# The RMS factor of four dense inputs, moved from the input to the evacuation, in a decoder step on one core

## What is computed

```python
def rms_norm(x, g):
    xf = x.astype(F32)
    y = xf * lax.rsqrt(jnp.mean(xf * xf, axis=-1, keepdims=True) + EPS)
    return (y * g.astype(F32)).astype(x.dtype)

def modulate(x, g, shift, scale):
    return rms_norm(x, g) * (1.0 + scale) + shift

def swiglu_ffn(h, w13, w2):
    a, b = jnp.split(h @ w13, 2, axis=-1)
    return (jax.nn.silu(a) * b) @ w2
```

## Time and profile before

| | us |
|---|---|
| median of 3 runs | 2125.33 (2123.13 to 2126.2) |
| the profiled execution | 2127.41 |
| its span, first to last instruction | 2125.8 |
| TensorE busy | 1877.3 (88%) |
| VectorE busy | 780.2 (37%) |
| ScalarE busy | 722.0 (34%) |
| GpSimd busy | 174.3 (8%) |

### The profile page before, as it was taken

How to read it: one execution, slowest core, us unless ns; L and a number is a source line. 1 busy time by engine, 2 the same in 40 slices (tenths; PEclk the granted TensorE clock), 3 DMA queues, 4 the chain that set the end, 5 groups by cost and what they waited for, 6 DMA issues and landing times.

```text
span 2125.8 us, 43188 instructions
## 1 busy us (share of the span) xinstructions
PE 1877.3 (88%) x17058; PEld 1647.2 (77%) x17058; DVE 780.2 (37%) x1200; ACT 722.0 (34%) x1056; POOL 174.3 (8%) x321
## 2 busy tenths in 40 slices
PE   4999995999999978979878988788769599999998
PEld 1647994999999978977433767677539599999997
DVE  3993333333322333156477222222223423333222
ACT  4432333333332223244333644344111333333222
POOL 2100122000000221010010000000004200000000
PEclk9899996999999988989677999999768799999999
DMA  8775321222222221212442899899851122222222
GB/s 233 261 265 177 95 86 30 79 84 84 79 68 81 82 86 50 79 50 90 133 134 90 272 393 349 322 345 381 318 186 50 35 84 79 85 83 67 82 81 72
DMA packets 245680, 302.86 MB, mean 142 GB/s; under 512 B 10451, under 2 KB 195774, under 8 KB 245438
## 3 DMA queue, kind: packets, MB, share of 16 engines
q1 hardware_dynamic: 241504, 292.14, 41.6%
q10 hardware_dynamic: 3142, 8.11, 1.1%
q0 software_dynamic: 928, 1.06, 0.2%
HBM read 293.89 MB, written 7.37 MB: 142 GB/s over the span
## 4 chain that ended last, share of the span: by engine, by line
PE 72%; DMA 8%; SPq 5%; DVE 4%; issue 4%; ACT 3%; POOL 2%; DVEq 0%; POOLq 0%; ACTq 0%
PE ps L538 54%; PE ps L464 5%; DMA kpg<-in_cache_k 4%; SPq L415 3%; PE ps L491 2%; SPq L422 2%; PE ps L778 1%; DMA vpg<-in_cache_v 1%; PE ps L829 1%; PE ps L926 1%; PE ps L815 1%; DMA xcm<-in_x_sample 1%; PE ps L684 1%; PE ps L767 1%; PE ps L677 1%
## 5 line engine op out<-in xcount | busy, mean ns | idle before, releaser
L538 PE MATMUL ps<-hr,ws 128*128 128x288 f32 x5760 | 796.7, 301 | 60.4 <-DVE hr L1838 60.4
L538 PEld LDWEIGHTS ps<-hr,ws 128*128 128x128 f32 x5760 | 787.9, 193 | 70.3 <-issue 37.4
L1832 DVE TENSOR_TENSOR ws<-raw,ws 128x1024 fp32r<-128x1024 f32 x200 | 234.8, 1175 | 715.4 <-ACT ws L1219 715.4
L1219 ACT ACTIVATE ws<-raw 128x1024 fp32r<-128x1024 f32 x200 | 201.5, 1009 | 709.6 <-PE ps L538 651.9
L538 PE MATMUL ps<-gr,ws 128*128 128x288 f32 x2112 | 281.9, 296 | 0.0
L538 PEld LDWEIGHTS ps<-gr,ws 128*128 128x128 f32 x2112 | 281.7, 189 | 0.0
L1399 ACT ACTIVATE kTs<-ps 128x512 f32<-128x512 f32 x256 | 140.0, 596 | 184.5 <-PE ps L464 184.3
L464 PE MATMUL ps<-identz,kpg 128*128 128x128 f32 x1024 | 147.3, 291 | 35.1 <-DMA kpg<-in_cache_k 33.8
L464 PEld LDWEIGHTS ps<-identz,kpg 128*128 128x128 f32 x1024 | 119.7, 149 | 59.5 <-ACT kTs L1399 29.5
L491 PE MATMUL ps<-raw,cond 128*32 128x256 f32 x896 | 87.5, 484 | 28.8 <-DMA raw<-in_w_ada_mix 23.3
L538 PE MATMUL ps<-hg,ws 128*128 128x288 f32 x768 | 104.1, 299 | 3.1 <-DVE mark L1825 3.1
(11 more groups left out here) (320 smaller groups left out, 1588.9 us busy)
## 6 DMA issues: line engine op xcount, KB each, us to landing
kpg<-in_cache_k SPq DMA_DIRECT2D x128, 512.0 KB, 5.8
vpg<-in_cache_v SPq DMA_DIRECT2D x128, 512.0 KB, 5.9
raw<-in_ffn_w SPq DMA_DIRECT2D x88, 512.0 KB, 3.8
raw<-in_w_ada_mix SPq DMA_DIRECT2D x48, 512.0 KB, 5.2
raw<-in_w_ada_ffn SPq DMA_DIRECT2D x48, 512.0 KB, 4.3
raw<-in_ffn_w SPq DMA_DIRECT2D x48, 384.0 KB, 3.3
raw<-in_w_ada_kv SPq DMA_DIRECT2D x16, 512.0 KB, 4.9
raw<-in_ssm_w_glu SPq DMA_DIRECT2D x16, 512.0 KB, 4.1
```

Of the source, the lines that this page charges most:

```text
L538: last = mm(ps[:, 4 * s + 2 * tile + h, 0:HALF], ws[:, wslot, w, k, :], src[:, k0 + k, v, h * HALF:(h + 1) * HALF], start=first, stop=(end ...
L1219: A(ws[:, w, 0, 0:nk, :].rearrange("p k n -> p (k n)"), raw[:, slot, 0:nk, :].rearrange("p k n -> p (k n)"), ACT.Copy).then_inc(slab_high, 1)
L1832: TT(f(ws[:, w, 1, 0:nk, :]), f(raw[:, slot, 0:nk, :]), f(ws[:, w, 0, 0:nk, :]).bitcast(F32), ALU.subtract).then_inc(raw_done[slot], 1)
```

## The change

With rms the root of the mean square of a token and r = 1/rms, the input of a dense layer is x * gain * r + shift for each token, so its product with a weight matrix W is r * (W (x * gain)) + W shift. The change multiplies by r, and adds W shift, when PSUM is emptied.

- The layer ahead makes the scaled tiles. As soon as tile k of x is updated in glu, down0 or wo, ScalarE makes the high part of x * gain for the prompt (`scale_high`), GpSimd the product for the 64 sample columns (`sample_scale`, ahead of the squares of the tile), and VectorE the low parts (`scale_low`). For q this is done within kv, a tile every second unit, into a second buffer `hr2`; wo's input also lies there.
- `hr` and `hr2` have 16 more columns, of which 10 are used: the nine shifts, and the first one again (`shift_high`, `shift_low`). In these four layers the matmuls of the second half have 298 columns instead of 288, so W shift comes out beside the product.
- The norm product is made by TensorE within the first units of the next layer: in up after 4 k tiles of the first unit's second slab (banks 6 and 7), in kv after 2 k tiles of the second unit (banks 2 and 3). Root and reciprocal follow within the first turn, which is written out ahead of the loop.
- In up, VectorE copies the shift columns, multiplies both PSUM pairs by `rstd`, adds the shifts of the samples to the gate; ScalarE makes Silu with the prompt's shift as its bias; VectorE adds the shift of the other pair within the product.
- In kv and q, ScalarE copies PSUM and the shift columns (into `lin`); GpSimd then multiplies each of the 16 + 8 tiles by `rstd` and adds the shifts (`scale_shift`). ScalarE's squares of the keys wait for the first 8 (`lin_ready`), TensorE's token transposes for 16, ScalarE's squares of the queries for their own.
- Several buffers lie elsewhere to make room. No DMA is added.

```diff
+                more = C9 + 1 if name in ("up0", "up1", "kv", "q") else 0
...
+                            if first and S == 2 and (u, j) == (1, 1):
+                                pe.wait_ge(norm_root, NORMS[name])
                             for k in range(nk):
+                                if first and S == 2 and (u, j, k) == (0, 1, 4):
+                                    pe.wait_ge(free[1], USES[name][1])
+                                    norm(NORMS[name], 6)
+                                if first and S == 1 and (u, k) == (1, 2):
+                                    norm(NORMS[name], 2)
...
+                                        wide = HALF + h * more
+                                        last = mm(ps[:, 4 * s + 2 * tile + h, 0:wide], ws[:, wslot, w, k, :],
+                                                  src[:, k0 + k, v, h * HALF:h * HALF + wide], start=start,
...
+            def scale_high(name, k, s):
+
+                n, m, dst = APPLY[name]
+                act.wait_ge(x_ready, (n + 1) * KD if name == "q" else n * KD + k + 1)
+                A(part(dst, k, 0)[:, 0:SEQ], tile(x, k)[:, 0:SEQ], ACT.Copy,
+                  scale=gain[:, m, ds(k, 1), 0:1].rearrange("p a c -> p (a c)"))
+                act.wait_ge(sample_scaled, SCALED[name] + k + 1)
+                A(part(dst, k, 0)[:, SEQ:T], scaled[:, s, :], ACT.Copy).then_inc(h_high, 1)
...
-                            A(halves(t1[:, s, :]), ps[:, 4 * s:4 * s + 2, 0:HALF], ACT.Silu).then_inc(e_ready, 1)
-                            act.wait_ge(free[s], uses(name, s, at) + 1)
-                            A(part(gr, f, 0), t2[:, s, :], ACT.Copy).then_inc(g_high, 1)
+                            act.wait_ge(gate_in, at)
+                            A(t1[:, s, 0:SEQ], t1[:, s, 0:SEQ], ACT.Silu, bias=shifts[:, s, 0, 0:1])
+                            A(t1[:, s, SEQ:T], t1[:, s, SEQ:T], ACT.Silu).then_inc(e_ready, 1)
+                            act.wait_ge(product, at)
+                            A(part(gr, k, 0), t2[:, s, :], ACT.Copy).then_inc(g_high, 1)
...
+            def sample_scale(name, k, s):
+
+                n, m, dst = APPLY[name]
+                pool.wait_ge(x_ready, (n + 1) * KD if name == "q" else n * KD + k + 1)
+                g = by_token(gain[:, m, ds(k, 1), 1:C9].rearrange("p a c -> p (a c)"))
+                pool.wait_ge(h_ready, READY[name] + k - 1)
+                TT(scaled[:, s, :].rearrange("p (b t) -> p b t", b=DB), sample(tile(x, k)), g, ALU.mult).then_inc(sample_scaled, 1)
...
+            def scale_shift(name, k, s, at, dst, row):
+
+                pool.wait_ge(free[s], uses(name, s, at) + 1)
+                t, sh = tile(dst, k), lin[:, ds(row, 1), :].rearrange("p a c -> p (a c)")
+                step(TT(t, t, rstd[:, :], ALU.mult))
+                TT(sample(t), sample(t), by_token(sh[:, 1:C9]), ALU.add)
+                TT(t[:, 0:SEQ], t[:, 0:SEQ], sh[:, 0:1].to_broadcast([P, SEQ]), ALU.add).then_inc(lin_ready, 1)
+
+            with pool.Fori(0, KD // 2) as i:
+                for u in range(2):
+                    sample_scale("q", i * 2 + u, u)
+            pool.wait_ge(rstd_ready, 2)
+            with step.loop(0, 4, 4) as i:
+                for u in range(4):
+                    scale_shift("kv", i * 4 + u, u % 2, i * 2 + u // 2, kvT, i * 4 + u)
...
+            def scale_low(name, k, s):
+
+                _, m, dst = APPLY[name]
+                dve.wait_ge(h_high, READY[name] + k + 1)
+                hi, lo = part(dst, k, 0), part(dst, k, 1)
+                STT(lo[:, 0:SEQ], tile(x, k)[:, 0:SEQ], gain[:, m, ds(k, 1), 0:1].rearrange("p a c -> p (a c)"), hi[:, 0:SEQ].bitcast(F32),
+                    ALU.mult, ALU.subtract)
+                TT(lo[:, SEQ:T], scaled[:, s, :], hi[:, SEQ:T].bitcast(F32), ALU.subtract).then_inc(h_ready, 1)
...
+                            CP(shifts[:, s], ps[:, 4 * s + 1:4 * s + 4:2, HALF:HALF + C9])
+                            by_norm = step.mark(TT(halves(t1[:, s, :]), ps[:, 4 * s:4 * s + 2, 0:HALF], halves(rstd[:, :]), ALU.mult))
+                            TT(halves(t2[:, s, :]), ps[:, 4 * s + 2:4 * s + 4, 0:HALF], halves(rstd[:, :]), ALU.mult).then_inc(free[s], 1)
+                            step.wait(by_norm)
+                            TT(sample(t1[:, s, :]), sample(t1[:, s, :]), by_token(shifts[:, s, 0, 1:C9]), ALU.add).then_inc(gate_in, 1)
...
+                            STT(t2[:, s, 0:SEQ], t2[:, s, 0:SEQ], shifts[:, s, 1, 0:1], t1[:, s, 0:SEQ], ALU.add, ALU.mult)
+                            TT(sample(t2[:, s, :]), sample(t2[:, s, :]), sample(t1[:, s, :]), ALU.mult).then_inc(product, 1)
```

More of the change, by code:

```diff
@@ L516, in dense, with turn @@
                 g0 = n0 - SLABS["glu"]
-                src = gr if name.startswith("down") else hg if name == "glu" else hr
+                src = gr if name.startswith("down") else {"glu": hg, "q": hr2, "wo": hr2}.get(name, hr)
+                more = C9 + 1 if name in ("up0", "up1", "kv", "q") else 0
                 kfirst = {"glu": 0, "up0": 8, "kv": 16, "q": 24, "wo": 32, "up1": 40}.get(name)
-                with pe.Fori(0, units // per) as i:
+                def turn(i, first=False):
                     for u in range(per):
@@ L1270, in dense, with turn @@
                 S, n0 = len(slabs), SLABS[name] - DENSE0
-                def turn(i, last):
+                def turn(i, last=False, first=False):
                     for u in range(per):
                         s = u % 2
+                        k = i * per + u
                         for j in range(S):
@@ L1283, in turn @@
                                 split(n0 + n + 2, i * (per * S), slabs[(j + 2) % S][2] if S == 4 and j < 2 else 8)
-                        at = i * (per // 2) + u // 2
+                            if first and S == 2 and n == 0:
+                                root(NORMS[name], 6)
                         if name == "glu":
@@ L1297, in turn @@
                             if not (last and u >= per - 2):
-                                square(kT, i * per + u + 2, s)
-                if tail:
-                    with act.Fori(0, units // per) as i:
-                        turn(i, False)
-                else:
-                    with act.Fori(0, units // per - 1) as i:
-                        turn(i, False)
-                    turn(units // per - 1, True)
+                                square(kT, k + 2, s)
+                        if name in ("glu", "down0", "wo"):
+                            scale_high(NEXT[name], k, s)
@@ L1308, in _ @@
+                lo, hi = int(name in NORMS), units // per - (0 if tail else 1)
+                if name in NEXT:
+                    shift_high(NEXT[name])
+                if lo:
+                    turn(0, first=True)
+                with act.Fori(lo, hi) as i:
+                    turn(i)
+                if not tail:
+                    turn(hi, last=True)
             dense("glu")
             act.wait_ge(put, 16 * 6)
-            root(1)
-            apply("up0")
             dense("up0")
@@ L1555, in _ @@
             back(backq, 2 * H, DK).then_inc(picks_ready, 1)
+            with step.loop(0, 4, 2) as i:
+                for s in range(2):
+                    scale_shift("q", i * 2 + s, s, i, qT, i * 2 + s + 2 * H)
             pool.wait_ge(head_ready, 2 + 2 * H)
@@ L1863, in dense, with turn @@
                 S, n0 = len(slabs), SLABS[name] - DENSE0
-                steps_ = per * {"glu": 1, "q": 1}.get(name, 0)
-                def turn(i, last):
+                steps_ = per * {"glu": 1, "q": 1, "up0": 2, "up1": 2}.get(name, 0)
+                def turn(i, last=False, first=False):
                     for u in range(per):
@@ L2073, in _ @@
             dense("wo")
-            root(3)
-            apply("up1")
             dense("up1")
```

206 lines of the change are left out of this document (100 added, 106 removed).

## The result

The changed kernel took 2030.01 us (median of four runs, 2025.17 to 2036.67), the kernel before 2124.23 us beside it: ratio 0.9557, 95% interval 0.9526 to 0.9588, so 94 us less. A second series gave 2027.16 us and 0.9544 (0.9520 to 0.9568). The prediction was 2040 us, 2017 to 2064.

The account below looks back on a forecast made before the run. The prediction took TensorE's dense layers, idling in a serial ladder between them, as the bound. 108.6 us left after the norm, less 11.3 for columns and 12 for GpSimd, gave 85.3 saved: 2040 us, range 2017 to 2064.

Parts of the forecast that it names:

- Boundaries: Pauses ahead of up0, kv, q and up1, 142 us in all, shrink to 7.0 to 7.9 us each: 112.3 us go.
- 2.6 us: Ahead of up0, kv and up1, time from the update of x to the last scaled tile being ready: 2.6 us.
- 1.00 through the four boundaries: Sign of the forecast: TensorE's granted clock stays at 1.00 at the boundaries to up0, kv, q and up1.
- The norm product: Now between matmuls in up0, kv and up1: three times 1.13 us, 3.4, plus 0.3 us lost waiting.
- Ten columns: Ten more columns in 2688 matmuls of up, kv and q cost 4.2 ns each, 11.3 us in all.
- The evacuation in up: Emptying PSUM in the up layers costs nothing: low part ends at 8.9 us, with 2.4 us to spare.
- The third rival: Evacuation in up overruns its 2.4 us, for instance by more table loads; 1 us over is 42 us: 2082 us, chance 0.07.
- GpSimd: the step that failed: GpSimd's factor and shifts on K, V and q tiles lose 12 us: 7 at q's first head product, 5 at q's end.
- if each VectorE instruction with two SBUF inputs stops it for its whole length: In kv, VectorE stops GpSimd 27% of the time, so K tiles are done 11.5 us after kv's end.
- the first of them: Rival: GpSimd keeps up, or the columns cost nothing: 2028 or 2029 us, with both 2017; chance 0.24.
- the forecast with 12 us: Main case: GpSimd's tiles in kv and q lose 12 us; 2040 us, within 2031 to 2054, chance 0.52.
- The second: Rival: VectorE's 3.75 us reciprocal in each q unit stops GpSimd too, leaving 42 us behind q: 2067 us, chance 0.10.

Follow-up runs that it names:

- x first: Changed kernel with VectorE updating x before its split in glu, down0 and wo, and glu's sigmoid ahead of ScalarE's split: 2027.13 us, ratio 0.9539.
- both halves wide: Changed kernel with both half-matmuls of each pair 298 columns wide instead of the second alone: 2048.37 us, ratio 0.9646.
- Without the cover: Changed kernel with TensorE waiting for all eight scaled tiles before the first matmul of up0, kv and up1: 2055.0 us, ratio 0.9662.

## Why the prediction was right, point by point

- **Boundaries: right, 3.3 us too good.** 112.3 us were to go; with GpSimd's 1.2 taken off q's boundary, 142.0 - 33.0 = 109.0 went. q's own came out at 7.74 (8.94 - 1.20) where 7.7 was predicted. At the other three, TensorE waited 1.95, 1.05 and 1.50 us for the last tile. A first step that failed is "2.6 us" from x to the last tile: it took 3.1, since I priced VectorE's two low parts at 0.75 and 0.22 without asking who runs beside them. GpSimd's squares of the same tile did, and the run without them has 0.75 and 0.22. That is 1.45 of the 3.3 us. The last six matmuls took 1.1 us to their answer, and 1.56 in up0, where I had 0.8: 1.4 more. And x of up1 came 4.07 us after the answer, not 3.6, as VectorE's split ahead of it took 1.80 us beside GpSimd's sum. The 1.56 is the clock, which fell after up0's wait, against "1.00 through the four boundaries": the 30 matmuls from there took 5.84 us, and 4.32 in the run without the last squares, where it stayed at 1.00.
- **The norm product: right.** It took 1.14 us, as its like in the earlier trace rows, and the slabs that hold it were 2.0, 1.0 and 1.0 us longer than a steady one (8.53, 7.49 and 7.46 against 6.50), 4.0 in all; 3.7 were put down. Some 1.1 of the 8.53 is the low clock again: with x first, where the clock stayed up, that slab took 7.41. So the norm itself is 2.9, and it came out near 3.7 by luck.
- **Ten columns: the right sum from two wrong terms, so luck.** I put 4.2 ns on a wide matmul; the up loops ran 135.4 against 133.2 or 133.3, which is 4.0 to 4.4, and 11 us as predicted. But the columns cost up to 6.7 each, 16 us by the slabs' answers and 18 by the counts, and the rows that were moved apart to make room for them gave 4 to 7 back. I took the 133 ns of a matmul as a property of its columns; in these runs it went with the place of its input as well. TensorE: Matmul & The Clock Gate, a page of the Trainium skill, section "Wait — 56ns, not 53.3ns?", has a warm matmul cost its columns at 2.4 GHz and a small constant; by estimate from that, ten columns are 4.2 ns. The runs here don't agree: 6.7 and 7.4, and those decide.
- **The evacuation in up: right.** A unit of up0, against the earlier trace rows:

```profile
462.25 1.06 ACT L1242 ACTIVATE ws<-raw 128x1024 fp32r<-128x1024 f32 x1 [5.35 <-PE ps L555]
...
468.93 0.76 DVE L1954 TENSOR_TENSOR gr<-t,gr 128x576 f32 x1 [0.99 <-ACT gr L1320]
469.95 1.23 DVE L1882 TENSOR_TENSOR ws<-raw,ws 128x1024 fp32r<-128x1024 f32 x1 [0.27 <-ACT ws L1242]
```

  The low part ends 7.4 us after the answer, where I had 8.9, as no table load stands in the loop any more, and TensorE has no gap in it. The third rival needed the opposite.
- **GpSimd: the step that failed.** I put 12 us on it; it was 1.2. Start (21.6 us before kv's end, 21 predicted) and a tile alone (2.95 us, 3.2) were near. What was wrong is "if each VectorE instruction with two SBUF inputs stops it for its whole length": that made eight tiles last 32.5 us, and they took 27.6. The two do shut each other out, as the earlier trace rows had it, and the timeline at kv's end shows it on both sides:

```profile
843.68 1.42 POOL L1576 TENSOR_TENSOR kvT<-kvT,rstd 128x576 f32 x1 [0.15 <-issue]
...
866.33 1.93 DVE L1882 TENSOR_TENSOR ws<-raw,ws 128x1024 fp32r<-128x1024 f32 x1 [4.95 <-ACT ws L1242]
...
867.14 2.41 POOL L1576 TENSOR_TENSOR kvT<-kvT,rstd 128x576 f32 x1
...
868.18 1.91 DVE L1898 SCALAR_TENSOR_TENSOR hr<-x,gain,hr  x1
...
870.21 1.03 POOL L1578 TENSOR_TENSOR kvT<-kvT,lin  x1
```

  VectorE's split took 1.93 us and not 1.23, its low part 1.91 and not 0.75; GpSimd's product 2.41 and not 1.43. The wait is shared: over the eight tiles GpSimd lost 4.0 us (27.6 against 8 x 2.95), and VectorE's instructions were 5.2 us longer than alone, off the path. I had given all of it to GpSimd. The K tiles were done 6.0 us after kv's end (11.5 predicted; of the 5.5 between, 2.9 are this, 2.0 the shorter tile and 0.6 the earlier start), the head product waited 1.20 us where I had 6 and a falling clock, and at q's end the last square stood 9.97 us after the last answer, as in the earlier trace rows, with the sums still the 9.61 us of before:

```profile
926.50 0.65 ACT L1329 ACTIVATE qT<-ps 128x576 f32<-128x576 f32 x1 [6.11 <-PE ps L555]
...
928.76 9.61 PE L788 MATMUL ps<-t,pickq 128*16 128x288 f32 x32 [2.30 <-ACT t L1286]
...
936.47 0.68 ACT L1286 ACTIVATE t<-qT 128x576 f32<-128x576 f32 x1 [0.29 <-PE ps L788]
```

- **The rivals.** What came is the first of them: GpSimd keeps up, 2028 us. I gave it 0.24 and the forecast with 12 us 0.52, so the likeliest case was not the one that came, though the range held it. The 1.2 us isn't fixed, though: the same wait was 2.2 us without the columns and 2.0 without them and with rows of 576, where kv is shorter, and none with both halves wide, where it is longer. The second, the reciprocal that stops GpSimd, falls by the timeline in q: a whole product of GpSimd's lies inside a reciprocal, at its usual length.

```profile
883.97 3.75 DVE L1911 RECIPROCAL t<-t 128x576 f32<-128x576 f32 x1
...
885.08 1.43 POOL L1576 TENSOR_TENSOR kvT<-kvT,rstd 128x576 f32 x1
```

  That is the rule of the Trainium skill, SBUF — State Buffer, section "Who interferes with whom", for one SBUF input, and the trace agrees.
- **The sum.** 109.0 - 4.0 - 11.1 - 1.2 = 92.7 us against 94.2 by the medians. The two spans differ by 102.2: the stretch from q's sixth answer to wo's first was 10.5 us shorter in the profiled execution after, glu 2.4 shorter and the front 4.9 longer, each within what they do from run to run.

## What to carry to other kernels

When a factor moves from a layer's input to its output, price first what becomes free to be made earlier: here that was 77 of 108 us, and the norm's own chain 31. Two engines that shut each other out share the lost time, so put it on the one that the path hangs on only after asking which of them has to wait. A term that comes out as predicted may still be two that cancel; taking the suspected cost out alone, and moving the data without it, told them apart.

## What the runs showed of the hardware that was not expected

- The same 288-column matmuls, at a granted clock of 1.00, took 131.9 to 132.2 or 133.0 to 133.3 ns in the up layers as the rows of their input lay 592 or 576 numbers apart. The inputs of glu and down still lie 576 apart; whether they would gain was not tried.
- Glu's matmuls, whose instructions on TensorE are the same in all these kernels, took 130.1 ns in some profiled executions (that of the changed kernel among them) and 133.3 in others, of the same kernel too (its second series); in the first the starts lie at 132 and 128 in turn, in the second at three times 131 and once 140. Wo's took 131.7, and 134.7 in the run with both halves wide. What decides this is open; over glu it is 2.4 us.
- Without the cover, 7.7 us without work were followed by 4 us in which TensorE's granted clock stood at 0.50. In the changed kernel's up0 a wait of 1.95 us was followed by a clock of 0.50 from 336 to 339 us, while waits of 1.05 and 1.50 us at kv and up1 left it at 1.00. The length of the wait doesn't settle it: in the run without GpSimd's tiles, 1.94 us at the same place left the clock at 1.00 (second slab 7.39 us, against 8.53).
